# Expert weights in groups of four neighbouring rows per partition, with 16 KB runs from expert 5 on

## The reference, cut to what matters

```python
def _expert_choice_ffn(u, w_router, w_g, w_u, w_d):
    b, n, _ = u.shape
    cap = CAPACITY_FACTOR * n // N_EXPERTS
    logits = jnp.einsum('bnd,de->ben', u, w_router, preferred_element_type=jnp.float32)
    aff = jax.nn.softmax(logits, axis=1)
    gate, idx = lax.top_k(aff, cap)
    bidx = jnp.arange(b)[:, None, None]
    xe = u[bidx, idx]
    hg = jnp.einsum('becd,edf->becf', xe, w_g)
    hu = jnp.einsum('becd,edf->becf', xe, w_u)
    ye = jnp.einsum('becf,efd->becd', jax.nn.silu(hg) * hu, w_d) * gate[..., None].astype(u.dtype)
    return jnp.zeros_like(u).at[bidx, idx].add(ye)
```

## Time and profile before

| what | value |
|---|---|
| time before, median of 3 runs | 2314.52 us (2312.52 to 2320.67) |
| the profiled execution | 2317.68 us |
| its span, first to last instruction | 2315.9 us |
| granted TensorE clock, mean | 0.969 |
| PE busy | 2015.6 us (87%) |
| PEld busy | 1379.1 us |
| DVE busy | 1118.0 us |
| moved by DMA | 757.58 MB, mean 327 GB/s |
| experts of layer 0 | about 1290 to 1731 us of the span |
| experts of layer 1 | about 1861 to 2304 us |

### The profile page before, as it was taken

How to read it: one execution, slowest core, us unless ns; L and a number is a source line. 1 busy time by engine, 2 the same in 40 slices (tenths; PEclk the granted TensorE clock), 3 DMA queues, 4 the chain that set the end, 5 groups by cost and what they waited for, 6 DMA issues and landing times.

```text
span 2315.9 us, 34904 instructions
## 1 busy us (share of the span) xinstructions
PE 2015.6 (87%) x13636; PEld 1379.1 (60%) x13636; DVE 1118.0 (48%) x1731; ACT 541.9 (23%) x838; POOL 71.6 (3%) x109
## 2 busy tenths in 40 slices
PE   7999999999999999999999986666679998666665
PEld 5999556999899845799886542222239753222222
DVE  3877777878877777887743211000017421100001
ACT  3333133433433223333423100000004210000001
POOL 0000000000000000000300000000000000000000
PEclk9999999999999999999999999999999999899988
DMA  9987876988689777788763899999998699999997
GB/s 347 334 295 261 314 255 214 294 311 302 226 286 322 253 292 255 232 308 313 251 246 104 352 419 421 422 422 422 422 408 281 259 394 421 421 422 422 422 422 317
DMA packets 240449, 757.58 MB, mean 327 GB/s; under 512 B 14016, under 2 KB 124256, under 8 KB 193136
## 3 DMA queue, kind: packets, MB, share of 16 engines
q1 hardware_dynamic: 233248, 737.33, 83.2%
q0 software_dynamic: 6864, 19.00, 2.6%
q10 hardware_dynamic: 256, 0.13, 0.0%
HBM read 755.22 MB, written 1.18 MB: 327 GB/s over the span
## 4 chain that ended last, share of the span: by engine, by line
PE 57%; DMA 32%; DVE 4%; SPq 3%; ACT 1%; issue 1%; DVEq 1%; ACTq 0%
DMA W<-in_w_exp_down 29%; PE psum L870 22%; PE psum L882 10%; PE psum L944 5%; PE psum L925 4%; PE psum L1412 3%; PE psum L1343 2%; SPq L592 2%; PE psum L1150 1%; PE psum L1302 1%; DMA W<-in_w_exp_up 1%; PE psum L787 1%; DMA W<-in_w_conv_in 1%; DMA W_mod<-in_mod_w 1%; PE psum L1324 1%
## 5 line engine op out<-in xcount | busy, mean ns | idle before, releaser
L870 PEld LDWEIGHTS psum<-parts 128*128 128x128 f32 x4224 | 517.8, 192 | 9.1 <-issue 1.9
L870 PE MATMUL psum<-parts 128*128 128x256 f32 x4224 | 521.1, 283 | 1.1 <-ACT parts L1448 0.8
L1302 PE MATMUL psum<-W,scr 128*32 128x512 f32 x1920 | 270.4, 687 | 165.6 <-DMA W<-in_w_exp_up 165.6
L1800 DVE SCALAR_TENSOR_TENSOR mod_acc<-W_mod,cond,mod_acc 128x1024 f32<-128x1024 f32 x196 | 251.8, 1285 | 45.0 <-issue 27.5
L2356 DVE TENSOR_TENSOR scr<-scr,psum 128x256 f32<-128x256 f32 x32 | 13.5, 422 | 530.5 <-ACT scr L1716 530.5
L882 PE MATMUL psum<-parts 128*128 128x512 f32 x1056 | 258.0, 393 | 0.2 <-DVE parts L1995 0.2
L1969 DVE TENSOR_TENSOR parts<-W,parts 128x1024 fp32r<-128x1024 f32 x176 | 207.2, 1220 | 70.2 <-ACT parts L1504 70.1
L1302 PEld LDWEIGHTS psum<-W,scr 128*32 128x32 f32 x1920 | 58.6, 117 | 305.3 <-issue 177.1
L882 PEld LDWEIGHTS psum<-parts 128*128 128x128 f32 x1056 | 192.5, 188 | 45.8 <-DVE parts L1982 7.8
L787 PE MATMUL psum<-k_ones,k_ident 128*128 128x256 f32 x736 | 206.2, 413 | 0.0
L787 PEld LDWEIGHTS psum<-k_ones,k_ident 128*128 128x128 f32 x736 | 135.0, 199 | 103.1 <-issue 89.7
(11 more groups left out here) (329 smaller groups left out, 1700.1 us busy)
## 6 DMA issues: line engine op xcount, KB each, us to landing
W<-in_w_exp_down SPq DMA_DIRECT2D x128, 1024.0 KB, 26.5
W_mod<-in_mod_w SPq DMA_DIRECT2D x123, 1024.0 KB, 6.5
W<-in_w_exp_up SPq DMA_DIRECT2D x120, 1024.0 KB, 26.3
W<-in_w_exp_gate SPq DMA_DIRECT2D x120, 1024.0 KB, 24.9
W<-in_ffn_w_gate SPq DMA_DIRECT2D x44, 1024.0 KB, 9.1
W<-in_ffn_w_up SPq DMA_DIRECT2D x44, 1024.0 KB, 11.6
W<-in_ffn_w_down SPq DMA_DIRECT2D x44, 1024.0 KB, 10.4
W<-in_w_in SPq DMA_DIRECT2D x24, 1024.0 KB, 8.6
```

The lines of the kernel that those rows point to most:

```text
L870: ins = pe.matmul(psum[:, 4 + t % 2, S * g:S * g + S], w[:, t % 2, g, kc, :], u[:, kc, :], start=(n == 0 and kc == 0), stop=(n == 2 and kc ...
L1302: ins = pe.matmul(psum[32 * q:32 * q + 32, 4, :].rearrange("p (g n) -> p g n", g=2), x, w[:, :, q, :], start=(b == 0), stop=(b == KC - 1), ...
L1800: ins = dve.scalar_tensor_tensor(acc[:, :], w, col, acc[:, :], mul, add)
```

## The change

Rows are now grouped by four: blocks 4g to 4g+3 share 512 neighbouring rows, and partition p holds rows 4p to 4p+3. From expert 5 on (`HALVES`) one DMA of 2 MB brings all four rows of a partition (16 KB in one piece) into two neighbouring slots, for gate, up and down. Experts 0 and 2 to 4 take the same rows as halves of a group: 1 MB, two of the four rows, 8 KB in one piece and then a gap of 8 KB. Expert 1 still takes single rows (4 KB), now one in four. The hidden columns are split differently over the four quarters q, since the down matrix's rows are grouped as well: a quarter takes pairs of neighbouring columns with a step of four. The tokens' columns are taken with a step of four instead of two, and the router's weights come in 32 DMAs of 32 partitions with a semaphore of their own instead of 8 of 64.

```diff
-PAIRED_COLUMNS = (7, 9)
+GROUPED_COLUMNS = (7, 9)
-def paired_rows(b):
-    return slice(2 * P * (b // 2) + b % 2, 2 * P * (b // 2 + 1), 2)
+def grouped_rows(b):
+    return slice(ROWS * P * (b // ROWS) + b % ROWS, ROWS * P * (b // ROWS + 1), ROWS)
...
-CONST2_LOADS = len(CONSTS2) - 1 + 4 * LAYERS
+CONST2_LOADS = len(CONSTS2) - 1
+ROUTER_LOADS = 16 * LAYERS
+ROWS = 4
+HALVES = 5
...
-            def pair_half(layer, e, n, pair, s):
-                sp.dma_start(part(W[:, s, :], 0, 2, D), gate_and_up[n][layer, ds(e, 1), 2 * P * pair:2 * P * pair + 2 * P, :]
-                             .rearrange("a (p j) n -> p (a j) n", j=2)).then_inc(landed[s], 16)
+            def half_group(layer, e, n, b):
+                s = gate_slot(b) + 2 * n
+                rows = gate_and_up[n][layer, ds(e, 1), ROWS * P * (b // ROWS):ROWS * P * (b // ROWS + 1), :]
+                sp.dma_start(part(W[:, s, :], 0, 2, D), rows.rearrange("a (p h j) n -> p (a h) j n", h=2, j=2)[:, b % ROWS // 2, :, :]
+                             ).then_inc(landed[s], 16)
+            def group(layer, e, n, g):
+                s = ROWS * g + 2 * n
+                rows = gate_and_up[n][layer, ds(e, 1), ROWS * P * g:ROWS * P * (g + 1), :]
+                sp.dma_start(W[:, s:s + 2, :].rearrange("p a b -> p (a b)"), rows.rearrange("a (p j) n -> p (a j n)", j=ROWS)
+                             ).then_inc(landed[s], 16)
...
+            def ring_down_group(layer, e, g, E):
+                sp.wait_ge(e_pe.s, e_pe.at(f"d{2 * g + 1}", E))
+                s = KC + 2 * g
+                rows = A["w_exp_down"][layer, ds(e, 1), 512 * g:512 * g + 512, :]
+                sp.dma_start(W[:, s:s + 2, :].rearrange("p a b -> p (a b)"), rows.rearrange("a (p j) n -> p (a j n)", j=ROWS)
+                             ).then_inc(landed[s], 16)
...
-            def ring_blocks(layer, e, pair, used, E):
-                sp.wait_ge(e_pe.s, e_pe.at(f"k{used}", E))
+            def ring_halves(layer, e, b, E):
+                sp.wait_ge(e_pe.s, e_pe.at(f"k{b + 1}", E))
                 for n in range(2):
-                    pair_half(layer, e, n, pair, 2 * ring_pair(2 * pair) + n)
+                    half_group(layer, e, n, b)
+            def ring_group(layer, e, g, E):
+                sp.wait_ge(e_pe.s, e_pe.at(f"k{ROWS * g + 3}", E))
+                for n in range(2):
+                    group(layer, e, n, g)
...
-                with sp.Fori(3, EXPERTS) as e:
-                    for pair in range(4):
-                        ring_blocks(layer, e, pair, 2 * pair + 1, e + (E0 - 1))
+                for e in range(3, HALVES):
+                    for b in range(0, KC, 2):
+                        ring_halves(layer, e, b, e + (E0 - 1))
                     for q in range(4):
                         ring_down(layer, e, q, e + (E0 - 1))
+                with sp.Fori(HALVES, EXPERTS) as e:
+                    for g in range(KC // ROWS):
+                        ring_group(layer, e, g, e + (E0 - 1))
+                    for g in range(2):
+                        ring_down_group(layer, e, g, e + (E0 - 1))
...
+            for l in range(LAYERS):
+                for h in range(ROWS):
+                    for j in range(ROWS):
+                        to = w_router[32 * h:32 * h + 32, l, :].rearrange("p (b j e) -> p b j e", j=ROWS, e=EXPERTS)
+                        of = A["w_router"][j::ROWS, l, :].rearrange("p (b h e) -> p b h e", h=ROWS, e=EXPERTS)
+                        pool.dma_start(to[:, :, j, :], of[:, :, h, :]).then_inc(router_landed, 16)
...
-                    turn_tile(15 + 4 * layer + t, t, paired=True)
+                    turn_tile(15 + 4 * layer + t, t, grouped=True)
...
-                        ins = pe.matmul(psum[:, FEW_BANKS[kc], 0:FEW], x_tok[:, t, paired_rows(kc)], sel[:, t, 0:FEW],
+                        ins = pe.matmul(psum[:, FEW_BANKS[kc], 0:FEW], x_tok[:, t, grouped_rows(kc)], sel[:, t, 0:FEW],
...
-                                w = W[:, s:s + 2, D * (b % 2):D * (b % 2) + D].rearrange("p g (q n) -> p g q n", q=4)
                             for q in range(4):
+                                w = part(spare[b], 0, 2, D) if extra else W[:, s:s + 3:2, D * (b % 2):D * (b % 2) + D]
+                                w = w.rearrange("p g (b n h k) -> p g b h n k", b=2, h=2, k=2)[:, :, q // 2, q % 2, :, :]
                                 ins = pe.matmul(psum[32 * q:32 * q + 32, 4, :].rearrange("p (g n) -> p g n", g=2),
-                                                x, w[:, :, q, :], start=(b == 0), stop=(b == KC - 1),
-                                                skip_group_check=True)
+                                                x, w, start=(b == 0), stop=(b == KC - 1), skip_group_check=True)
```

More of the change, by code:

```diff
@@ L435, in expert_landed @@
         def expert_landed(layer, s, e, first):
+            if s % 2 and not first:
+                e = min(e, HALVES - 1) if isinstance(e, int) else HALVES - 1
             return e * 16 + (slot_landed(f"moe{layer}", s) - (16 if s < KC and not first else 0))
@@ L833, in turn_tile @@
                     c = P * (kc % 4)
-                    rows = paired_rows(kc) if paired else slice(P * kc, P * kc + P)
+                    rows = grouped_rows(kc) if grouped else slice(P * kc, P * kc + P)
                     ins = pe.transpose(psum[:, 4 + 2 * t + kc // 4, c:c + P], x_tok[:, t, rows], ident[:, :])
@@ L1283, in gate_up @@
                         else:
-                            s = 2 * (b // 2) if first else 2 * ring_pair(b)
+                            s = gate_slot(b)
                             if not first and b in (4, 6):
@@ L1288, in gate_up @@
                                 for n in range(2):
-                                    pe.wait_ge(landed[s + n], expert_landed(layer, s + n, e, first))
-                        if extra and b == 7:
-                            for n in range(2):
-                                for q in range(4):
-                                    w = last_gate[:, q, :] if n == 0 else last_up[0][:, q, :] if q < 3 else last_up[1]
-                                    ins = pe.matmul(psum[32 * q:32 * q + 32, 4, 256 * n:256 * n + 256], x, w,
-                                                    start=False, stop=True, skip_group_check=True)
-                        else:
-                            if extra:
-                                w = part(spare[b], 0, 2, 4, 256) if b < 6 else spare[b].rearrange("p (g q) n -> p g q n", g=2)
-                            else:
-                                w = W[:, s:s + 2, D * (b % 2):D * (b % 2) + D].rearrange("p g (q n) -> p g q n", q=4)
+                                    pe.wait_ge(landed[s + 2 * n], expert_landed(layer, s + 2 * n, e, first))
@@ new lines, in gate_up @@
+                        if extra and b >= 6:
+                            for q in range(4):
+                                for r in range(2):
+                                    c = 2 * (q // 2) + r
+                                    to = psum[32 * q:32 * q + 32, 4, :].rearrange("p (g n) -> p g n", g=2)[:, :, P * r:P * r + P]
+                                    if b == 6:
+                                        w = spare[b].rearrange("p (g q) (n h k) -> p g q h n k", g=2, h=2, k=2)[:, :, c, q % 2, :, :]
+                                        ins = pe.matmul(to, x, w, start=False, stop=False, skip_group_check=True)
+                                        continue
+                                    for n, w in enumerate((last_gate[:, c, :], last_up[0][:, c, :] if c < 3 else last_up[1])):
+                                        ins = pe.matmul(to[:, n, :], x, w.rearrange("p (n h k) -> p h n k", h=2, k=2)[:, q % 2, :, :],
+                                                        start=False, stop=True, skip_group_check=True)
+                        else:
@@ L1315, in gather_some @@
                     for t in range(TT):
[L1316 removed]
+                        ins = pe.matmul(psum[:, kc % 4, FEW:SOME], x_tok[:, t, grouped_rows(kc)], sel[:, t, FEW:SOME],
                                         start=(t == 0), stop=(t == TT - 1))
```

42 lines of the change are left out of this document (19 added, 23 removed).

## The result

The changed kernel takes **2332.53 us** (median of 7 runs, 2327.61 to 2333.59) against 2316.76 us (7 runs, 2312.52 to 2324.18) on the same chips: ratio **1.0066, 95% interval [1.0051, 1.0081]**. It is slower by 0.66%, where a gain of 4.4 us was forecast with a range of 2302 to 2321 us. The profiled execution took 2331.67 us with a span of 2329.9 us; the kernel before had 2317.68 and 2315.9.

The account below looks back on a forecast made before the run. The prediction took the DMA engines to bound the experts, with TensorE waiting. Its terms, -10.0 + 1.5 + 4.1 = -4.4 us on 2314.52 us, gave 2310.1 us, range 2302 to 2321 us.

Parts of the forecast that it names:

- Term 1: Experts 5 to 15 in both layers: 16 KB runs save 0.456 us per expert, together -10.0 us.
- Term 2: End of layer 1's experts: the last 2 MB landing delays the final down work, +1.5 us; layer 0's end is covered.
- Term 3: Start of each layer's plateau: step-four x_tok reads slow transposes and first gather, delaying the first ring DMA, +4.1 us.
- At nothing: Router DMAs, expert 1's last blocks, slower later gathers and later SyncE waits: all taken as covered, 0 us.
- what PE loses inside a plateau costs nothing: In both layers' expert stretches DMA sets the pace and TensorE waits, so TensorE's losses there add 0 us.
- 26.5 us of queue: In the expert plateaus data lands 26.5 us after SyncE issues it, taken as cover for later waits.
- PE late throughout because of a lower clock: Rival, in the plateaus: TensorE's clock falls in its long pauses and makes it late; no size given, chance 0.05.
- a stretch of the first plateau under 410 GB/s: Layer 0's experts: a DMA rate this low was named as a sign that the forecast is wrong.

Follow-up runs that it names:

- e7: e1 with the 16 KB runs taken away, all experts loaded in 8 KB runs or shorter; 2318.54 us, ratio 1.0003 to the kernel before.
- e2: The kernel before with only the step of the x_tok columns changed from two to four; 2337.44 us, ratio 1.0090 to the kernel before.
- e4: The changed kernel with expert 1's last two blocks multiplied in 4 and 8 matmuls as before; 2329.60 us, ratio 1.0056 to the kernel before.
- e1: The changed kernel with x_tok stored in blocks, so TensorE reads it without a step; 2312.24 us, ratio 0.9976 to the kernel before.
- e6: The changed kernel with step four kept only in the second and third gather, not transposes and first gather; 2318.95 us, ratio 1.0012 to the kernel before.
- e9: The changed kernel with its second gather streaming 256 columns per weight load instead of 64; 2330.27 us, ratio 1.0067 to the kernel before.

## Why the prediction was wrong

*Term 1* was right: 428 GB/s, 29.34 us per expert against 29.37, and 8.9 us by e7, where 22 experts less the two ends were to give 8.5.

*Term 2* was right: 2316.70 - 2313.01 = 3.7 us from landing to L1397, forecast 3.6; and TensorE was still waiting for the last piece, by 0.84 us where the margin was worked out as 0.9. In layer 0 the chain behind the experts goes through the convolution's weights (15.2 us of `W<-in_w_conv_in`), as the cover of that end supposed.

*Term 3* had the right mechanism and was too small. The 12 records took 3.06 us (forecast about 2.9), but from the first gather to the first ring load 8.0 us passed instead of 4.3, in both layers: +3.7 us each, not 2.06. About 1.9 are the 16 records; most of the rest are the two gate/up blocks behind them, which ran at the lower clock (1.94 us for 8 records against 1.06). Where the clock stayed at 1.00 at this place, in layer 0 of e2 and of e4, 6.1 and 6.2 us passed, which is the term as forecast; that the clock would fall there was not thought of. Together +7.4 in place of +4.1.

The Trainium skill's rule on cachelines (Advanced Engine Details and Errata, section Memory Cachelines), that two hits on a 16-byte line are wanted for full speed, agrees with the gathers' load rows: 192 ns unstepped, 196 at step two, 330 at step four. The transposes' loads in the earlier trace rows don't agree, 141 ns at step one and 209 at step two. The largest single piece of T's growth, 3.7 us in the second gather, lies where that load, not the stream, sets the pace.

**The step that failed** is a sentence under "At nothing": "`gather_some` slows down, inside a plateau in which DMA is full", with its ground in the first part, "what PE loses inside a plateau costs nothing". I had taken 26.5 us of queue from the earlier trace rows as cover. That is a median over the settled experts, in which TensorE waits. In experts 0 and 1 the cover is T against 29.7 us, and the kernel before had 2.1 us of it. The rows of the kernel before would have shown this: 12 MB, the issue of expert 2's down held until the 16 records that start at 1321.39 are through, the first ring load at 1293.83. With them most of the cost could have been worked out even at the full clock: 1.8 us for the first gather's later records and 3.5 for the second gather (16 and 32 records at the 0.110 us more that Term 3 already had), less 2.1 of cover, is 3.2 us a layer, and the sum would have been -10.0 + 1.5 + 4.1 + 6.4 = +2 us. The pieces and the strided stream of expert 1, at nothing in the same sentence of the prediction, are 1.8 us more (T is 29.3 us in e1, 27.6 before): 5.0 us a layer and +5.6 us in all. The lower clock behind the loads brought the two gaps to 8.65 and 6.9 us.

The new sum: -10.0 + 1.5 + 7.4 + 15.55 = +14.5 us, where the two layers show +17.1. (The profiled executions differ by only 14.0 us, since the changed one reached its first gather 3.2 us earlier: the kernel before had its clock at 0.50 in the router's stage of layer 0 and the changed one didn't.) The 2.6 us left are not settled. Two things bear on them. From 1300 to 1310 the changed kernel moved 374 and 354 GB/s at a DMA share of 0.99 and 1.00, where the kernel before moved 424 and 433; at 424 GB/s that is an estimate of 1.5 us. The other kernels with a stepped first gather show it as well (e2 388 and e4 359 GB/s from 1300 to 1305), those without don't (e1 428, e6 429); no run says why. And e7, with neither the step nor the long runs, still takes 1.6 us more in its two layers than the kernel before. Of the rivals, none was this case. "PE late throughout because of a lower clock" named the clock but put it in TensorE's long pauses inside the plateau. The sign given as what would make the forecast wrong, a stretch of the first plateau under 410 GB/s, is the one that came.

## What to carry to other kernels

Ask what covers a slower engine at the place itself, not in the settled loop. At the head of a prefetched stream the cover is the bytes that the queue can hold before its next in-order wait, divided by the rate, less the time to the instruction that releases it.

When rows are regrouped to make transfers longer, someone reads the other operand with that step. If it is the stationary operand, store it in the order in which it is loaded: here a VectorE instruction already there did it, at about 0.5 us more for each of two tiles in a layer, and turned a loss of 0.66% into a gain of 0.24%.

Median and total of a run hide what two effects do to each other; durations between two events of the same program, beside the ratio, told the parts apart. They come from one execution each, so look first at whether the difference lies where the edit reaches: in e4 and e9 about a third of it did not.

## What the runs showed of the hardware

- Loading 128x128 f32 weights took 192 ns unstepped, 196 at step two and 330 at step four; in a row of small matmuls the pace was 0.118 us a record at step two and 0.240 at step four, and nearly the same whether the granted clock was 1.00 throughout or fell to 0.50 on the way (7.84 and 7.73 us for 32).
- The granted clock fell to 0.50 during the row of stepped loads with 64 columns each, and stayed at 1.00 with 256 columns each.
- In the router's stage the clock fell in some executions and not in others, and a stretch that took 114.0 us took up to 119.6 us with it; with five matmuls in the waits it stayed at 1.00 and five runs lay within 1.5 us, with two it fell to 0.50 and ten runs lay within 10.1 us.
- A moving operand read in pairs with a gap between them took 637 ns where a contiguous one took 617 (512 columns, medians).
- With the DMA engines full, 16 KB runs moved 428 GB/s and 8 KB runs 422 (e1 and e7); the page counts one packet for a run of either length.
- A VectorE instruction over 128x1024 f32 that turned the columns by fours took 1300 ns in place of 811.
